# Hybrid mixer of a two-block model: convolution units first in the input projection, softmax in two halves, attention rows last in the output projection

## The reference, cut to what matters

```
def hybrid_mixer(h, w_in, ..., w_out):
    p = h @ w_in
    gq, gk, gv, gr, glr, ca, cg, sq, sk, sv = jnp.split(p, offsets, axis=-1)
    glog = jax.nn.log_sigmoid((glr @ gla_w_gate2 + gla_b_gate)) / GLA_TAU
    o_gla = gla_group(gq, gk, gv, glog, gr, gla_norm_g)      # gated linear attention, 4 heads
    o_conv = conv_group(ca, cg, conv_w, conv_b, ln_g, ln_b)  # GLU, 31-tap causal conv, LayerNorm, swish
    o_swa = swa_group(sq, sk, sv, swa_sinks)                 # window attention, 8 heads, softmax with a sink
    return jnp.concatenate([o_gla, o_conv, o_swa], axis=-1) @ w_out
```

## Time and profile before

| | |
|---|---|
| median of 3 runs | 1563.46 µs (1563.1 to 1578.05) |
| the profiled execution, its own time | 1560.63 µs |
| its span, first to last instruction | 1558.8 µs |
| busy share of the span | PE 94%, DVE 63%, ACT 49%, POOL 5% |
| mean granted TensorE clock | 0.970 |
| first mixer, PE's first product to the next feed-forward part's first | 707.15 to 838.73 µs |
| second mixer, the same | 1230.23 to 1362.24 µs |

### The profile page before, as it was taken

The page is one execution under the profiler, slowest core; times in us unless marked ns, Lnnn a source line. Parts: engine busy times, 40 slices in busy tenths (PEclk is TensorE's granted clock), DMA queues, the critical chain, the costliest instruction groups (busy, mean ns, idle before and its releaser), DMA issues. The chain is left out here.

```text
span 1558.8 us, 21614 instructions
## 1 busy us (share of the span) xinstructions
PE 1462.1 (94%) x8968; PEld 1281.2 (82%) x8968; DVE 986.9 (63%) x1192; ACT 764.7 (49%) x1016; POOL 76.1 (5%) x77
## 2 busy tenths in 40 slices
PE   6999999899999899998859999999999885999998
PEld 6999999799987788878847888878888785878886
DVE  6766786588855566555856665556654486665644
ACT  4433753455544544443765444454444368454433
POOL 0000000000000000000510000000000032000000
PEclk9999999899999999998989999999999897999999
DMA  7644465666655555454324665546555450465543
GB/s 250 213 132 138 141 204 174 168 175 183 189 189 162 178 186 189 162 176 109 109 69 135 217 187 180 186 149 216 187 176 189 109 149 15 139 207 176 189 154 107
DMA packets 254357, 255.87 MB, mean 164 GB/s; under 512 B 24483, under 2 KB 217396, under 8 KB 254260
## 3 DMA queue, kind: packets, MB, share of 16 engines
q1 hardware_dynamic: 253376, 252.21, 51.4%
q10 hardware_dynamic: 884, 2.28, 0.4%
HBM read 253.42 MB, written 1.05 MB: 163 GB/s over the span
## 5 line engine op out<-in xcount | busy, mean ns | idle before, releaser
L967 DVE TENSOR_TENSOR w_lo<-raw,w_hi 128x2048 fp32r<-128x2048 f32 x240 | 550.8, 2297 | 337.7 <-ACT w_hi L583 337.5
L583 ACT ACTIVATE w_hi<-raw 128x2048 fp32r<-128x2048 f32 x240 | 458.4, 1912 | 352.6 <-PE stream L1636 153.1
L1636 PE MATMUL stream<-a_hi,w_hi 128*128 128x256 f32 x1056 | 305.8, 290 | 10.9 <-DVE a_lo L986 7.2
L1636 PE MATMUL stream<-a_lo,w_hi 128*128 128x256 f32 x1056 | 303.3, 287 | 0.0
L1636 PE MATMUL stream<-a_hi,w_lo 128*128 128x256 f32 x1056 | 302.8, 287 | 0.0
L1636 PE MATMUL stream<-w_hi,a_hi 128*128 128x512 f32 (+2 forms) x672 | 254.4, 379 | 7.4 <-DVE w_lo L967 7.4
L1636 PE MATMUL stream<-w_hi,a_lo 128*128 128x512 f32 (+2 forms) x672 | 249.5, 371 | 0.0
L1636 PE MATMUL stream<-w_lo,a_hi 128*128 128x512 f32 (+2 forms) x672 | 248.9, 370 | 0.0
L1636 PEld LDWEIGHTS stream<-a_hi,w_hi 128*128 128x128 f32 x1056 | 207.0, 196 | 13.3 <-issue 7.6
L1636 PEld LDWEIGHTS stream<-a_lo,w_hi 128*128 128x128 f32 x1056 | 207.4, 196 | 0.0
L1636 PEld LDWEIGHTS stream<-a_hi,w_lo 128*128 128x128 f32 x1056 | 207.2, 196 | 0.0
(11 more groups left out here) (283 smaller groups left out, 1686.3 us busy)
## 6 DMA issues: line engine op xcount, KB each, us to landing
raw<-in_ffn_w_up SPq DMA_DIRECT2D x136, 512.0 KB, 5.0
raw<-in_ffn_w_down SPq DMA_DIRECT2D x104, 512.0 KB, 4.5
raw<-in_ffn_w_gate SPq DMA_DIRECT2D x88, 512.0 KB, 4.0
raw<-in_w_in SPq DMA_DIRECT2D x80, 512.0 KB, 4.7
raw<-in_w_out SPq DMA_DIRECT2D x24, 512.0 KB, 4.5
raw<-in_w_in SPq DMA_DIRECT2D x20, 256.0 KB, 4.0
raw<-in_w_ret_o SPq DMA_DIRECT2D x8, 512.0 KB, 4.0
raw<-in_w_lru_o SPq DMA_DIRECT2D x8, 512.0 KB, 4.4
```

The lines of the kernel that those rows point to most:

```text
L583: nc.scalar.activation(w_hi[s][:, :, :], raw[s][:, :, :], ACT.Copy).then_inc(w_hi_ready, 1)
L967: V.tensor_tensor(w_lo[s][:, :, :], raw[s][:, :, :], w_hi[s][:, :, :].bitcast(F32), ALU.subtract).then_inc(w_split, 1)
L1636: return nc.tensor.matmul(dst, lhs, rhs, start=start, stop=stop, skip_group_check=True)
```

## The change

The order of the first four units becomes: cm `ca`, cm+1 `cg`, cm+2 `glr`, cm+3 `gq` and `gk`. The rest keep their places. The three engines' code in the mixer is reordered with it:

- PE: unit cm is multiplied alone (before, two units were interleaved by k). The gate's product `z` stands inside unit cm+3, the products into `psm` inside unit cm+5 (before, ahead of it). The cross product stands ahead of unit cm+8, the first `gla_scores` inside it. The value products of the linear attention come straight after `gla_scores(1)`, then the transposes of the first softmax half (into `psm`). The transposes of the second half stand behind the first pass of the output projection, the window attention's value products (all heads, into `stream[0:2]`) behind the second.
- DVE: the softmax's maximum, shift and reciprocal are made in halves (`softmax_shift(b)`, `softmax_sums(b)`), seven small instructions more in a layer; `conv` steps come earlier.
- ACT: `products` from just after `hi(cm + 4)`; exponentials, normalising and copies in halves. Taps 24 to 30 (`products(TAPS)`) come behind the exponentials of the second half and `hi(cm + 10)`.
- POOL: four odd sums ahead of the two `ek` products, ten behind.
- Output projection: `WIDE_ORDER` takes the place of `MIX_ORDER`: the first two units read k = 0 to 3 (linear attention and convolution), the last two k = 4 to 7.

No product is added or removed on PE, and the weights read are the same.

```diff
-(PSM_SWA, PSM_GLA, PSM_CROSS, PSM_L) = (0, 2, 4, 5)
+(PSM_SWA, PSM_CROSS, PSM_GLA, PSM_L) = (0, 2, 3, 5)
@@ SP
-                for u, (n, m) in enumerate(MIX_ORDER):
+                for u, (n, m) in enumerate(WIDE_ORDER):
@@ POOL
+                odd_sums(1, 5)
                 for t in range(TT):
-                    pool.wait_ge(group_evac, g_mix + 2)
+                    pool.wait_ge(group_evac, g_mix + 4)
...
+                odd_sums(5, ODD_SUMS + 1)
@@ ACT
+                hi(cm + 3)
+                act.wait_ge(group_evac, gm + 2)
+                nc.scalar.activation(th2[:, :, :], th2[:, :, :], ACT.Tanh, scale=0.5).then_inc(glu_th, 1)
+                hi(cm + 4)
+                products(2)
+                act.wait_ge(ps7_full, ps70 + PS7_Z + 1)
...
+                hi(cm + 5)
+                products(6)
+                hi(cm + 6)
+                products(10)
+                hi(cm + 7)
+                products(12)
                 act.wait_ge(lev_ready, l + 1)
...
-                products(8)
+                products(18)
                 hi(cm + 8)
-                products(16)
+                products(24)
+                exponentials(0)
                 hi(cm + 9)
-                products(24)
...
+                normalise(0)
+                exponentials(1)
                 hi(cm + 10)
...
                 products(TAPS)
...
+                turned_probabilities(0, [psm[:, m, :] for m in range(3)])
+                normalise(1)
+                act.wait_ge(ps7_free, ps70 + PS7_PV + 1)
+                nc.scalar.activation(sq2[:, :, :], og[:, :, :], ACT.Square).then_inc(og_sq, 1)
...
+                hi(cm + 11)
                 operand_hi(b_hi[:, 0:2, :], hn[:, 0:2, :], op(op0 + 1))
...
+                turned_probabilities(1, [stream[m][:, :] for m in range(3)])
@@ DVE
+                lo(cm + 7)
+                conv(3)
                 read_pair(5, qs[:, 0:2, :], SWD ** -0.5)
...
                 ins.then_inc(qe_ready, 1)
-                conv(1)
+                conv(2)
+                window_scores(0)
                 lo(cm + 8)
-                conv(2)
                 read_pair(6, qs[:, 2:4, :], SWD ** -0.5)
+                softmax_shift(0)
                 conv(2)
                 window_scores(1)
...
+                softmax_shift(1)
...
+                dve.wait_ge(psm_full, psm0 + PSM_CROSS + 1)
+                V.tensor_copy(s_cross[:, :, :], psm[:, :, 0:P]).then_inc(psm_free, 1)
+                softmax_sums(0)
+                gla_scores(0)
+                lo(cm + 9)
                 gla_scores(1)
                 read_pair(8, gr[:, :, :], 1.0)
+                softmax_sums(1)
+                lo(cm + 10)
...
                 operand_lo(b_lo[:, 0:2, :], hn[:, 0:2, :], b_hi[:, 0:2, :])
+                lo(cm + 11)
                 dve.wait_ge(silu_th, l + 1)
@@ PE
+                psm_ready(PSM_L)
+                pe.wait_ge(group_evac, gm + 8)
                 pe.wait_ge(ps7_free, ps70 + PS7_PV)
...
+                probabilities(0, [psm[:, m, :] for m in range(3)])
...
+                pe.wait_ge(pt_free, 2 * l + 1)
+                for step, (c, t) in enumerate(tail_passes(range(cm + 9, cm + 13))):
+                    n, m = WIDE_ORDER[c - cm - 9]
...
+                    if step == 0:
+                        probabilities(1, [stream[m][:, :] for m in range(3)])
+                    if step == 1:
+                        pe.wait_ge(pt_free, 2 * l + 2)
+                        window_out()
```

More of the change, by code:

```diff
@@ L276, in build, with mx_half @@
         cg, cub = gu[:, :, 0, :], gu[:, :, 1, :]
+        def mx_half(row, b):
+            return mx[:, row, :].rearrange("p (a s) -> p a s", a=2)[:, :, 4 * b:4 * b + 4]
         th_t = gu[:, :, :, :].rearrange("p s a n -> p (s a) n")
@@ L532, in _, with odd_sums @@
                 nc.gpsimd.memset(up[:, :, 0:TAPS - 1], 0.0).then_inc(zeroed, 1)
+                def odd_sums(n, to):
+                    for k in range(n, to):
+                        m = 1 if k == 1 else k
+                        pool.wait_ge(tap_product, TAPS * l + 2 * m + 2)
+                        if k > 1:
+                            pool.wait_ge(odd_sum, ODD_SUMS * l + k - 1)
+                        nc.gpsimd.tensor_tensor(y_pool, odd[:, 0] if k == 1 else y_pool, odd[:, m % RING], ALU.add).then_inc(odd_sum, 1)
+                odd_sums(1, 5)
                 for t in range(TT):
-                    pool.wait_ge(group_evac, g_mix + 2)
+                    pool.wait_ge(group_evac, g_mix + 4)
                     pool.wait_ge(e_ready, TT * l + t + 1)
@@ L923, in _ @@
                 operand_hi(b_hi[:, 2:4, :], hn[:, 2:4, :], op(op0 + 2))
-                hi(cm + 11)
+                turned_probabilities(1, [stream[m][:, :] for m in range(3)])
+                for m in range(2):
+                    operand_hi(b_hi[:, 4 + 2 * m:6 + 2 * m, :].rearrange("p f n -> p (f n)"), stream[m][:, :], (pv_full, l + 1))
                 hi(cm + 12)
@@ L1497, in _ @@
+                conv(1)
+                lo(cm + 5)
                 dve.wait_ge(ez_ready, l + 1)
@@ L1605, in _ @@
                 operand_lo(b_lo[:, 2:4, :], hn[:, 2:4, :], b_hi[:, 2:4, :])
-                lo(cm + 11)
+                for m in range(2):
+                    operand_lo(b_lo[:, 4 + 2 * m:6 + 2 * m, :].rearrange("p f n -> p (f n)"), stream[m][:, :],
+                               b_hi[:, 4 + 2 * m:6 + 2 * m, :].rearrange("p f n -> p (f n)"))
                 lo(cm + 12)
@@ L2028, in _, with window_out @@
                 ins.then_inc(ps7_full, 1)
-                def window_out(heads):
-                    for h in heads:
+                probabilities(0, [psm[:, m, :] for m in range(3)])
+                cbank = stream[2]
+                pe.wait_ge(group_evac, gm + 9)
+                pe.wait_ge(yc_ready, l + 1)
+                for f in range(2):
+                    ins = mm(cbank[:, T:2 * T], means[:, 1:2].broadcast_to([P, P]), yc[0][:, f, :], f == 0, f == 1)
+                ins.then_inc(conv_full, 1)
+                def window_out():
+                    for h in range(SWH):
                         f, part = h // 2, slice(SWD * (h % 2), SWD * (h % 2) + SWD)
```

216 lines of the change are left out of this document (92 added, 124 removed).

## The result

| | before | after |
|---|---|---|
| median | 1566.13 µs (1563.1 to 1578.05, 4 runs) | 1599.49 µs (1599.02 to 1600.63, 4 runs) |
| ratio to before | | 1.0225, 95% interval 1.0187 to 1.0263 |
| span of the profiled execution | 1558.8 µs | 1597.2 µs |
| mean granted TensorE clock | 0.970 | 0.954 |
| first mixer, turn to turn | 131.2 µs | 150.6 µs |

The change makes the kernel slower, by 1.9 to 2.6% (ratio 1.0225); whether by more than 2% these runs do not tell. 1595 was forecast, 1566 to 1610 the range. "Turn to turn" is the measure used from here on: from PE's transposes of `x_t` ahead of the mixer to those behind it (`psm<-keep,x_t`, then `stream<-keep,x_t`), so that what differs outside does not enter. Together the mixers are 38.7 µs longer, and the span 38.4: all of it lies there.

A forecast was written before the change was run, and what follows sets the result against it. A mixer was taken as bound by a chain between DVE, ACT and POOL, not by PE. Projection end 14.6 plus clock 2 made 16.6 µs a mixer, twice 33; on 1560.63 this gave 1594, then 1596, stated as 1595, range 1566 to 1610.

The forecast's parts named there:

- Step 1: Gate: POOL's first four sums delay DVE's gate chain by 3.0 µs, to 744.9; PE waits 3.3 µs.
- Step 2: First window scores: POOL gets in between DVE's operations, query result at 759.6; PE waits 5.4 µs, bounds 0 and 5.4.
- Step 3: Second window scores: 8.3 µs of DVE with 5.2 of POOL's sums between, to 773.1; PE waits 6.0 µs.
- Step 4: Linear attention: DVE's first `gla_scores` waits for ACT's tap 24 until 792.0; PE waits 8.3, then 6.0 µs.
- Step 5: Linear attention's value products end at 807.8, now 807.4: up to here the change is worth nothing.
- step 8: Clock: half clock after waits hits value products and first passes, 0 to 4 µs a mixer, taken as 2.
- Step 6: Tail: square of `og` 5.5 µs later, remainders for k = 2, 3 ready at 826.7, now 820.65; first pass waits.
- Step 7: Output projection: first pass ends at 828.2, the rest at 853.3 against 838.7, 14.6 µs more.
- One sign: If right, 45 to 47 µs from the end of the value products to the next part, now 31.3.
- Rival C: Mixer's waits really go, value products end before 793; mixer 16 µs less, 1531 µs in all; chance 0.11.
- Rival B: POOL and DVE don't collide in the new order; mixer 3 µs longer, 5 with the clock, 1572; chance 0.18.

The follow-up runs named there:

- experiment 1: The kernel after with POOL's odd sums cut to 2 of 256 columns: 1585.63 µs, mixers 143.8 and 143.9 µs.
- Experiment 6: The kernel after with ACT's taps 24 to 27 moved earlier, ahead of the second half's exponentials: 1588.71 µs, mixers 144.4 and 143.5 µs.
- Experiments 4: The kernel after with the second half's normalising put ahead of the first half's copies on ACT: 1589.55 µs, mixers 144.1 and 144.1 µs.
- 5: The kernel after with DVE's `lo(cm+11)` moved behind the convolution's rows: 1594.74 µs, mixers 148.4 and 147.8 µs.
- 7: The kernel before with only the output projection's row order turned, attention rows last: 1572.97 µs, mixers 136.3 and 136.9 µs.
- Experiment 3: The kernel after with idle products on PE ahead of the second linear attention scores and the value products: 1586.91 µs, mixers 143.8 and 143.8 µs.
- experiment 12: The kernel of experiment 11 with 34 more idle products in the wait between the two sets of transposes: 1556.53 µs, ratio to before 0.9962.
- experiment 11: The kernel before with ACT's order changed and idle products ahead of the second window scores and first transposes: 1570.91 µs, ratio to before 1.0054.
- experiment 2: The kernel before with POOL's odd sums cut to 2 of 256 columns: 1561.29 µs, mixers 128.0 and 135.4 µs.
- experiment 8: The kernel after with normalising first, `lo(cm+11)` behind and taps 24 to 27 early, all together: 1576.16 µs, ratio to before 1.0091.

## Why the prediction was right

The time (1599.5 against 1595) and the sign were right, and so was the order of events in the mixer. But two terms were off in opposite directions, and that the sum came out so near is luck. Point by point:

- **Step 1, gate: right.** `glog` ready at 744.6 (forecast 744.9), PE waits 2.7 (3.3). The gate's chain lost 2.7 µs to POOL, partly in instructions of one operand (`TENSOR_SCALAR` 1.04 and 1.27, alone 0.30 and 0.29), which I had counted as free.
- **Step 2, first scores: wrong, 5.4 µs.** There is no such wait: the query result is out at 755.7, not 759.6. The gate products ran at half clock (5.41 instead of 3.67), so ACT and then POOL had `ek` 2 µs later than in my walk, at 751.3. By then DVE was through its `lo` and in two of the three sums; only the third took 2.15. The rule that a waiting POOL gets in between two of DVE's did not hold here: the first `ek` was issued before the second sum began (751.64), and both sums took 0.69. The collision fell on `qe` and the sums behind it, where PE had six microseconds of work to do. I had taken the upper bound of a term whose lower bound, 0, was the truth; which of the two holds is decided by 2 µs, as experiment 1 shows: with the gate 2.4 earlier, `ek` falls on the three sums (6.26) and PE waits 3.9.
- **Step 3, second scores: the wait right (6.1 against 6.0)**, its time 3.7 early, from step 2. Of the 11 µs that POOL was to cost in steps 2 and 3, 7.0 came.
- **Step 4, linear attention: right.** DVE waits 4.68 for ACT's tap inside the first `gla_scores`; PE waits 7.5 and 5.0 (8.3 and 6.0), all some 4 µs early. Experiment 6 shows that the tap is the cause.
- **Step 5, "worth nothing up to here": right by two errors.** Its own account does not balance: 17.8 go out (13.0, 1.8 and 3) and 23.0 come back; the walk's times, not this sum, carry the forecast. The value products start at 798.7, 4.4 ahead of the walk (step 2), and take 7.93 instead of 4.6 (step 8). Their end, 806.6, is 1.2 from the forecast.
- **Step 6, tail: right.** The square of `og` at 813.63 (forecast 813.7). `og` on DVE is at 821.7 instead of 818.9, all of these 2.8 µs from statistics and `keep_warm` at half clock. Experiments 4, 5 and 7 show the order's part: 2.8 of wait for normalising ahead of the square, 1.2 of wait for `lo(cm+11)` (2 to 3 with the clock), 5 with the clock for the rows' order.
- **Step 7, projection:** seven passes, transposes and window products took 25.6 from the end of the first pass, against 25.1. One sign did not come: from the end of the value products to the next part it is 51.3 µs, not 45 to 47. The clock makes up the most of it.
- **Step 8, clock: right in kind, mis-sized.** Forecast 2 µs a mixer, at most 4. By the rows: gate products 1.7, value products 3.3, transposes 1.3, statistics and `keep_warm` 2.8, second half of the first pass 1.3, second transposes 1.1. The price of 0.19 µs a product was read too low as well: the count of 16 in 3 µs takes in products that only overlap the window, and the rows of `before` at 0.50 stand 0.21 apart. Experiment 3 gives it as a whole, for two of the waits: 7. I had counted the products right behind a wait, and taken the rest as back at full speed. In fact the clock stayed at 0.50 through all 8 µs of value products, and over the short waits and small products behind them, to the first pass.

So the sum (33 µs against 39 in the mixers, 38 in the span) is right within its range because errors of opposite sign met: of the clock's terms 10 µs lie on the path of a mixer behind step 4, 8 more than forecast, against 4.4 too much for POOL (step 2) and 0.8 of small ones. 2.8 µs a mixer is what is left over. Rival C did not come: the value products ended at 806.6, not before 793. Rival B is priced too low by what experiment 1 shows: without POOL's sums a mixer is 12.6 µs longer than before, not 5. Its exact case was not run, as the `ek` products still held PE for 3.9 there; even with all of that wait taken off, 8.7 are left.

On POOL and DVE the prediction drew on the Trainium skill, GPSIMD Engine Reference, section 1. Specifications. It names, beside two SBUF inputs, a 2-port mode of DVE as what contends. The trace fits it: the `TENSOR_SCALAR` instructions with one input in SBUF took 1.04 and 1.27 µs beside POOL, and 0.30 and 0.29 without it, while the `RECIPROCAL`, also of one input, took 1.75 in both. Which mode each was in, no run here shows. I had read only the half of the sentence about two inputs.

The Trainium skill, TensorE: Matmul & The Clock Gate, section HAM oscillation — how this bites in real kernels, tells of a kernel whose matrix engine idled between its bursts of products, so that each burst began at the slow clock, and advises to restructure such a loop so that the engine stays busy. The runs here agree, at 7 µs of 150 (experiment 3), and at 7 of 136 for a single wait of 4.4 µs (experiment 12).

## What to carry to other kernels

A new wait in front of TensorE can cost its length and then the half clock behind it: price the products after the wait, all of them up to the next dense stretch, at 1.2 GHz as the first case and at 2.4 as the exception. A shorter wait can cost more than the longer one that it replaces, if short waits follow it; and idle products in a wait that can't be removed can be worth more than a better order. They are not worth it in every wait: in two waits of the kernel with ACT's new order they gave nothing (experiment 11), in the third 7 µs a mixer. Where an order of work moves a first consumer (here the output projection's first rows) to the result that is made last, everything that stood between in the other engines' queues comes onto the path.

## What the runs showed of the hardware that was not expected

- Behind most of the long waits the granted clock was 0.50 at once, but not behind all: after 4.05 µs in experiment 3 the next eight products took 1.20 and 1.08 in the two mixers, near their full speed of 1.05, and only the eight behind them 1.85. When it comes back is not set by the wait alone either. Twelve transposes behind a wait of 13.0 µs were followed by full speed in the kernel before, and those behind one of 13.9 µs by over 20 µs at half in the second mixer of experiment 2. In experiment 8 two passages with the same instructions and the same wait of 0.47 ran at 1.86 and at 1.05. What decides it was not settled.
- The value products of the linear attention (40 small products) did not bring the clock back in 7.9 µs of unbroken work in any of the runs in which they started at half. Of the 56 idle products of 256 columns in the first mixer of experiment 11, the first ran at 0.53 to 0.62 (780 to 784) and the others at 1.00. The 34 of experiment 12 ran at full speed from the first (4.32 µs) and kept it: the next transposes took 1.53.
- POOL's additions held up some DVE instructions with one operand in SBUF too: `TENSOR_SCALAR` took 1.0 to 1.3 instead of 0.3 µs, `RECIPROCAL` its usual 1.75.
- A faster chain can meet another collision: with POOL's sums nearly gone, three sums of DVE took 6.26 µs beside the two `ek` products, against 1.29 and 2.15 with them.
